# Two transformer blocks on one core: who sums the modulation, where latents and keys are turned, and in which order the mixers' outputs are normed

## The reference

```
c_act = silu(c)                                     # one row of 1024
mod   = c_act @ w_ada + b_ada                       # w_ada: 1024 x 6144
shift1, scale1, gate1, shift2, scale2, gate2 = split(mod, 6)
h     = rms_norm(x, g_mix) * (1 + scale1) + shift1
q_a, lat, k_r, iq, ik, iw, q_b, k_b, v_b, f_b = split(h @ w_in)
o_a   = dsa_attention(rope(q_a), rms_norm(lat, g_kv), rope(k_r), rope(iq), rope(ik), iw)
        # index scores: sum over 8 heads of iw * relu(iq . ik); the best 128 keys are kept
o_b   = forgetting_attention(q_b, k_b, v_b, f_b + b_forget)
mixed = concat(rms_norm(o_a, g_out_a), rms_norm(o_b, g_out_b))
x     = x + gate1 * (mixed @ w_out)
x     = x + gate2 * peer(rms_norm(x, g_ffn) * (1 + scale2) + shift2)
out   = rms_norm(x, g_final)
```

## Time and profile before

| | |
|---|---|
| runs | 3534.08, 3538.93, 3541.27 us; median 3538.93 |
| the profiled execution | 3541.71 us, its span 3539.9 |
| granted TensorE clock, mean | 0.972 |
| busy: TensorE, weight loads, VectorE, ScalarE, GpSimd | 94, 83, 76, 40, 29% |
| DMA | 855.56 MB, 242 GB/s over the span |

### The profile page before, as it was taken

One profiled execution on the slowest core, in us unless ns is written; L12 is line 12 of the kernel. 1 busy time (PEld: TensorE's weight loads), 2 busy tenths in 40 slices (PEclk: granted clock), 3 DMA queues, 4 the chain that ended last, 5 costly groups with the idle time before them and its releaser, 6 DMA issues. The chain is left out here.

```text
span 3539.9 us, 46446 instructions
## 1 busy us (share of the span) xinstructions
PE 3338.2 (94%) x18703; PEld 2946.8 (83%) x18703; DVE 2672.7 (76%) x4561; ACT 1400.4 (40%) x1899; POOL 1031.9 (29%) x652
## 2 busy tenths in 40 slices
PE   8997899999999998999999899889999999999998
PEld 7967558889999898788887786789999898888887
DVE  4458654349999895788888497549999896788888
ACT  4322452233333574233333345333333575333333
POOL 6516700002444330333332000002443331333332
PEclk9998999999999999999999899899999999999999
DMA  6313313237898899899997120226888899999996
GB/s 227 108 51 140 109 54 119 90 99 263 301 326 306 297 345 326 321 359 360 363 360 276 54 72 7 84 73 240 313 314 311 290 349 326 350 362 359 360 361 248
DMA packets 330506, 855.56 MB, mean 242 GB/s; under 512 B 22258, under 2 KB 188066, under 8 KB 297139
## 3 DMA queue, kind: packets, MB, share of 16 engines
q1 hardware_dynamic: 256562, 584.12, 47.1%
q0 software_dynamic: 73728, 268.47, 20.7%
HBM read 746.58 MB, written 105.93 MB: 241 GB/s over the span
## 5 line engine op out<-in xcount | busy, mean ns | idle before, releaser
L293 PE MATMUL ps<-ht_hi,parts 128*128 128x384 f32 (+2 forms) x5088 | 1373.8, 348 | 38.5 <-DVE parts L276 38.1
L276 DVE TENSOR_TENSOR parts<-ring,parts 128x2048 fp32r<-128x2048 f32 (+1 forms) x317 | 741.9, 2340 | 357.0 <-ACT parts L268 356.7
L293 PEld LDWEIGHTS ps<-ht_hi,parts 128*128 128x128 f32 x5088 | 936.6, 191 | 85.7 <-DVE parts L276 48.9
L268 ACT ACTIVATE parts<-ring 128x2048 fp32r<-128x2048 f32 (+1 forms) x317 | 606.7, 1914 | 831.7 <-PE ps L1525 677.2
L293 PE MATMUL ps<-ht_lo,parts 128*128 128x384 f32 (+2 forms) x2544 | 877.5, 345 | 0.0
L1888 POOL DMA_INDIRECT scr<-in_p_rows_u,cst x256 | 403.3, 1575 | 885.9 <-DVE scr L1758 563.9
L335 ACT ACTIVATE scr<-ps 128x384 f32<-128x384 f32 (+2 forms) x497 | 244.4, 505 | 942.0 <-PE ps L293 879.6
L1888 POOL DMA_INDIRECT scr<-in_peer_v,cst x256 | 375.3, 1466 | 770.2 <-DVE xres L1775 620.3
L1525 PE MATMUL ps<-parts,ht_lo 128*128 128x512 f32 x2304 | 530.2, 390 | 6.5 <-DVE ht_lo L1852 6.5
L1525 PE MATMUL ps<-parts,ht_hi 128*128 128x512 f32 x2304 | 529.3, 390 | 4.5 <-DVE ht_hi L1852 4.5
L1525 PEld LDWEIGHTS ps<-parts,ht_lo 128*128 128x128 f32 x2304 | 434.4, 189 | 97.3 <-DVE ht_lo L1852 6.9
(11 more groups left out here) (255 smaller groups left out, 2787.4 us busy)
## 6 DMA issues: line engine op xcount, KB each, us to landing
ring<-in_peer_u SPq DMA_DIRECT2D x128, 1024.0 KB, 6.8
ring<-in_peer_v SPq DMA_DIRECT2D x128, 1024.0 KB, 7.5
hbuf<-scr SPq DMA_DIRECT2D x128, 384.0 KB, 7.0
gbuf<-scr SPq DMA_DIRECT2D x96, 512.0 KB, 8.6
scr<-gbuf SPq DMA_DIRECT2D x64, 768.0 KB, 9.3
scr<-hbuf SPq DMA_DIRECT2D x64, 768.0 KB, 11.9
ring<-in_w_in SPq DMA_DIRECT2D x35, 1024.0 KB, 5.4
xres<-in_w_ada SPq DMA_DIRECT2D x18, 1024.0 KB, 7.4
```

What stands on the lines that cost most here:

```text
L268: e.activation(halves(m)[0], slot_view(m)[:, 0:units[m][0]], ACT.Copy).then_inc(A.sem, A.up(("hi", m)))
L276: e.tensor_tensor(lo, slot_view(m)[:, 0:units[m][0]], hi.bitcast(F32), ALU.subtract).then_inc(V.sem, V.up(("lo", m), ("slot", m)))
L293: ins = e.matmul(ps, l, r, start=(i == 0), stop=(i == n - 1))
```

## The change

**Modulation.** w_ada is laid out anew, as 6 groups of 1024 columns by 8 chunks of 128 rows: 48 pieces of 128x1024 (0.5 MB). Of a group VectorE multiplies piece 0 by a column of c and adds the other seven with one instruction each (`ada_dve`); eight matmuls of one column then sum over the partitions (`ada_pe`), and the bias is added a group at a time (`ada_sums`). Pieces 0 to 23 go with the eight units gq 0 to gv 3, three a unit; 24 to 47 with gb 0 to wo 2, two to four a unit, one beside each of wb. On VectorE they stand right behind the split of the next unit. GpSimd has no part of it, and the sliding stage none either. A load waits for the piece four before it.

**Mixers.** The positions come first on SP's queue, the sines and angles behind unit m2 0, latents' squares, index queries, latents and keys beside qa 0, the queries' rotation behind qa 1, and their turned copies behind the first block of index scores.

**Norm of the outputs.** Squares, root and turn by block: the squares of blocks 3, 2, 1 and 0 at iterations 11, 13, 15 and 17 of the loop, three roots at 16. wo2 0 takes the blocks as 3, 2, 1, 0; the loads of x and gate wait for the last scores instead of the last output.

```
-            for s in range(ADA_2):  ada_pool(e, w, s)          # gla_pool; sliding_pool likewise
+        ADA_GLA = {("gq", 0): (0, 3), ("gq", 1): (3, 6), ("gk", 0): (6, 9), ("gk", 1): (9, 12),
+                   ("gv", 0): (12, 15), ("gv", 1): (15, 18), ("gv", 2): (18, 21), ("gv", 3): (21, 24)}
+        ADA_JOIN = {("gb", 0): (24, 26), ("gb", 1): (26, 30), ("gb", 2): (30, 34), ("gb", 3): (34, 38),
+                    ("wb", 0): (38, 39), ("wb", 1): (39, 40), ("wb", 2): (40, 41), ("wb", 3): (41, 42),
+                    ("wo", 0): (42, 44), ("wo", 1): (44, 46), ("wo", 2): (46, 48)}
+        def ada_load(e, w, s):
+            if s >= 24:      w.wait_ge(*at_point("pv_pe", NB - 1))
+            if s % 24 >= 4:  w.wait_ge(*at_point("ada_used", s - 4))
+            e.dma_start(ada_in(s), inp["w_ada_2"][s])...
+        def ada_dve(e, w, span):
+            for s in range(*span):
+                cc = s % NC
+                w.wait_ge(*at_point("c_act")); w.wait_ge(*at_point("ada", s))
+                if cc == 0:
+                    if s % 24: ada_sums(e, w, s // NC - 1)
+                    ins = e.tensor_scalar(acc, ada_in(s), ct[:, 0:1], None, ALU.mult)
+                else:
+                    w.wait_ge(*V.now())
+                    ins = e.scalar_tensor_tensor(out=acc, in0=ada_in(s), scalar=ct[:, cc:cc + 1], in1=acc, ...)
+                ins.then_inc(V.sem, V.up(("ada_used", s)))
+        def ada_pe(e, w, k):
+            ps = bank(w, ("mods", k))
+            w.wait_ge(*at_point("ada_used", 8 * k + 7))
+            for j in range(8):  e.matmul(ps[:, j:j + 1], ada_acc(8 * k)[:, 128 * j:128 * j + 128], one, ...)
 # gla_pe, join_pe: where TensorE sums the groups
                     cols_major(e, w, (name, s, 0), v, 0)
+                    if (name, s) == ("gk", 0):  ada_pe(e, w, 0)
                     cols_major(e, w, (name, s, 1), v, 128, ("used", m))
+                    if (s, blk) == (1, 1):  ada_pe(e, w, 1)     # gv
+                    if (s, blk) == (3, 2):  ada_pe(e, w, 2)     # gv
+                if s == 2:  ada_pe(e, w, 3)                     # gb, between its two halves
+                if s == 1:  ada_pe(e, w, 4)                     # behind wb 1
+                    if (s, blk) == (2, 2):  ada_pe(e, w, 5)     # wo
 # gla_dve (gk, gv and join_dve likewise)
                     split_lo(e, w, U[name, s] + 1)
+                    ada_dve(e, w, ADA_GLA[name, s])
                     put_dve(e, w, (name, s, 1), dst[:, 2 * s + 1, :], psum((name, s, 1)), (name, "dve"))
 # mixers_dve
-            angles_dve(e, w)
             for (name, s), n, dst in m2_parts:
                 split_lo(e, w, U[name, s] + 1)
+                if (name, s) == ("qa", 0):  turned_keys(e, w)   # rotations of iq, k_r, ik; latents; copies
                 for blk in (1, 3):
                     put_dve(...)
+                if (name, s) == ("m2", 0):  angles_dve(e, w)
 # mixers_act: sines behind split_hi in m2 1, latent_squares in qa 0, and
+                if i in (11, 13, 15, 17):  mixed_squares(e, w, 3 - (i - 11) // 2)
+                if i == 16:
+                    for blk in (3, 2, 1):  mixed_root(e, w, blk)
 # mixed_pe
+            for blk in (3, 2, 1):  mixed_turn(e, w, blk)
+            for blk in (3, 2, 1, 0):
+                w.wait_ge(*at_point("ht", "mix", blk))
+                rows_major(e, w, ("wo2", 0, blk), v, 256, blk, ...)
+                if blk == 3:  mixed_turn(e, w, 0)
 # mixed_act
+            mixed_high(e, w, 3)
+            mixed_root(e, w, 0)
+            for blk in (2, 1, 0):  mixed_high(e, w, blk)
 # mixed_dve
+            for blk in (3, 2, 1):  mixed_mean(e, w, blk)
+            for blk in (3, 2, 1):  mixed_row(e, w, blk)
+            mixed_low(e, w, 3)
+            mixed_mean(e, w, 0)
+            mixed_row(e, w, 0)
+            for blk in (2, 1, 0):  mixed_low(e, w, blk)
```

More of the change, by code:

```diff
@@ L542, in ada_pool @@
[L542 to L570, removed]
@@ new lines, in ada_loads @@
+        def ada_loads(e, w, span):
+            for s in range(span[0] + 4, span[1] + 4):
+                if s // 24 == span[0] // 24:
+                    ada_load(e, w, s)
+        def ada_dve(e, w, span):
+            for s in range(*span):
+                cc = s % NC
+                acc = ada_acc(s)
+                w.wait_ge(*at_point("c_act"))
+                w.wait_ge(*at_point("ada", s))
+                if cc == 0:
+                    if s % 24:
+                        ada_sums(e, w, s // NC - 1)
+                    ins = e.tensor_scalar(acc, ada_in(s), ct[:, 0:1], None, ALU.mult)
+                else:
+                    w.wait_ge(*V.now())
+                    ins = e.scalar_tensor_tensor(out=acc, in0=ada_in(s), scalar=ct[:, cc:cc + 1], in1=acc, op0=ALU.mult,
+                                                 op1=ALU.add)
+                ins.then_inc(V.sem, V.up(("ada_used", s)))
@@ new lines, in ada_sums @@
+        def ada_sums(e, w, k):
+            cols = slice(8 * k, 8 * k + 8)
+            w.wait_ge(*at_point("ps", ("mods", k)))
+            w.wait_ge(*at_point("ada_bias"))
+            e.tensor_tensor(md[:, cols], psum(("mods", k))[:, 0:8], bd[:, cols], ALU.add).then_inc(
+                V.sem, V.up(("free", ("mods", k)), ("mod_done",)))
+        def ada_pe(e, w, k):
+            ps = bank(w, ("mods", k))
+            w.wait_ge(*at_point("ada_used", 8 * k + 7))
+            for j in range(8):
+                ins = e.matmul(ps[:, j:j + 1], ada_acc(8 * k)[:, 128 * j:128 * j + 128], one, start=True, stop=True)
+            ins.then_inc(P.sem, P.up(("ps", ("mods", k))))
@@ L580, in ada_turn @@
         def ada_turn(e, w):
-            for part in range(2):
-                w.wait_ge(*at_point("mod_done", part))
+            w.wait_ge(*at_point("mod_done"))
             ps = bank(w, ("modt",))
             e.transpose(ps[0:48, 0:128], md, ident).then_inc(P.sem, P.up(("ps", ("modt",))))
-        U = number
         def gla_sp(e, w):
@@ L2227, in mixers_act, with latent_squares @@
                     ins.then_inc(A.sem, A.up(("exp2", i)))
+                if i in (11, 13, 15, 17):
+                    mixed_squares(e, w, 3 - (i - 11) // 2)
+                if i == 16:
+                    for blk in (3, 2, 1):
+                        mixed_root(e, w, blk)
+        def latent_squares(e, w):
+            w.wait_ge(*at_point("m2", "act"))
+            w.wait_ge(*at_point("m2", "dve"))
+            for blk in range(NB):
+                if blk:
+                    w.wait_ge(*A.now())
+                e.activation(SCW[:, 0:128], M2[:, blk, 0:128], ACT.Square, accum_out=ssl[:, blk:blk + 1]).then_inc(
+                    A.sem, A.up(("squares", "lat")))
+            root_act(e, w, "lat", ssl)
         def latent_act(e, w, i):
@@ L2451, in mixed_act, with mixed_mean, mixed_row @@
             for s in range(4):
                 split_hi(e, w, U["wo2", s] + 1)
[L2454 to L2456 removed]
+        def mixed_mean(e, w, blk):
+            s = ssm[:, 2 * blk:2 * blk + 2]
+            w.wait_ge(*at_point("squares", "mix", blk))
+            e.tensor_scalar(s, s, 1.0 / 512, EPS, ALU.mult, ALU.add).then_inc(V.sem, V.up(("mean", "mix", blk)))
+        def mixed_row(e, w, blk):
+            s = ssm[:, 2 * blk:2 * blk + 2]
+            w.wait_ge(*at_point("root", "mix", blk))
+            e.reciprocal(s, s).then_inc(V.sem, V.up())
@@ L2467, in mixed_dve @@
-            mixed_low(e, w, NB - 1)
+            for k in range(2):
+                mv = MIX[:, blk, 512 * k:512 * k + 512]
+                e.scalar_tensor_tensor(out=mv, in0=mv, scalar=s[:, k:k + 1], in1=go[:, 512 * k:512 * k + 512],
+                                       op0=ALU.mult, op1=ALU.mult).then_inc(V.sem, V.up(("mix_normed", blk)))
+        def mixed_dve(e, w):
+            for blk in (3, 2, 1):
+                mixed_mean(e, w, blk)
+            for blk in (3, 2, 1):
+                mixed_row(e, w, blk)
+            mixed_low(e, w, 3)
+            mixed_mean(e, w, 0)
+            mixed_row(e, w, 0)
+            for blk in (2, 1, 0):
+                mixed_low(e, w, blk)
```

282 lines of the change are left out of this document (134 added, 148 removed).

## The result

| | before | after |
|---|---|---|
| median of 4 runs | 3536.5 us (3529.9 to 3541.3) | 3481.0 us (3480.2 to 3485.5) |
| ratio | | 0.9847, 95% interval 0.9828 to 0.9866 |
| the profiled execution, its span | 3541.7, 3539.9 us | 3481.2, 3479.4 us |
| granted TensorE clock, mean | 0.972 | 0.982 |

What follows compares the result with a forecast made beforehand. TensorE, busy 94% of the span, was taken as the bound, with time won only at its waits and low clock. Gains 25.9 + 16.5 + 12.8 = 55.2 off 3541.7, less 2.8, gave 3483.7, said as 3483; range 3465 to 3502 (0.67).

Steps and rivals of the forecast that it cites:

- The step for (gk, 0): First projections: TensorE stands still 7.6 us for VectorE's eighth modulation sum; with 3.0 of low clock, a loss of 10.6.
- (gb, 2): Join: the fourth group of column sums waits 2.1 us for VectorE, 3.1 with low clock (0 to 5).
- (gr, 1): The wait for GpSimd at 140 us goes, a 5.5 us wait for this unit's split comes; gain 1.5 (0 to 5).
- The sliding stage: Without GpSimd's sums and their DMAs: projections 100.4 to 71.4 us, gain 29.0; attention blocks gain 16.7.
- The low clock behind the stalls: First projections and join: 3.0 us lost behind the 7.6 us wait, 1.0 behind the 2.1 us wait.
- VectorE's 48 instructions: First projections and join: 58 us of sums on VectorE, costing nothing as such beside TensorE's work, 58 without that cover.
- Mixers: Latents and keys turned beside the query units: first relu from 2022.24 to 2002.9 us; gain 16.5 (10 to 18).
- Norm by blocks: Norm of the mixers' outputs: first wo2 matmul comes 14.3 us earlier; gain 12.8 (7 to 15).
- b: VectorE becomes the bound in the sliding projections and beside (qa, 0): gain 20 less, 3504 us (3502 to 3520); chance 0.19.
- c: Whole kernel: more comes back, no clock is lost behind the new waits, 3460 us; chance 0.06.
- d: First projections and join: w_ada loads delay the units' weights if DMA carries under some 160 GB/s, 3551 us; chance 0.04.
- e: First projections and join: DMA traffic, not GpSimd, stretches VectorE, 1 us in each of 17 units, 3500 us; chance 0.04.

Runs made afterwards that it cites:

- sum_early: Changed kernel with w_ada pieces 6 and 7 summed ahead of the four gate instructions, piece 8 alone in (gk, 0)'s iteration: 3467.8 us, 0.9804 to before.
- best: sum_early plus (gr, 1)'s split ahead of exps and products, and the fourth column sums behind (gb, 2): 3456.3 us, 0.9771 to before.
- pool_light: Kernel before, GpSimd doing only the last add of each sliding-stage modulation step; loads, waits and column matmuls stay: 3497.1 us, ratio 0.9887.
- pool_busy: Changed kernel with GpSimd's products and halvings put back as idle work on leftovers, without loads; gates' products of n=2 and 3 wait: 3535.5 us.
- dve_extra: Changed kernel with 5.2 us of idle VectorE work behind each split in the iterations of sqkv 1 to 5: 3505.4 us.
- m_only: Kernel before with only the modulation part of the change: median 3515.2 us, ratio 0.9936.
- l_only: Kernel before with only the mixers' latents and keys part of the change: median 3523.6 us, ratio 0.9959.
- n_only: Kernel before with only the norm by blocks: median 3525.5 us, ratio 0.9964.

## Why the prediction was right

**The new stalls by order came out to the tenth.** The step for (gk, 0) went through VectorE's queue: gate instructions to 59.8, split to 63.2, two sums to 65.8, TensorE from 58.2: 7.6 us. The timelines of VectorE and TensorE after:

```profile
57.26 2.53 DVE L764 SCALAR_TENSOR_TENSOR scr<-ps,scr 128x512 f32<-128x512 f32 x4 [8.88 <-ACT scr L716]
60.90 2.29 DVE L276 TENSOR_TENSOR parts<-ring,parts 128x2048 fp32r<-128x2048 f32 x1 [1.11 <-ACT parts L268]
63.31 2.69 DVE L548 SCALAR_TENSOR_TENSOR scr<-xres,scr 128x1024 f32<-128x1024 f32 x2
```
```profile
66.05 3.57 PE L564 MATMUL ps<-cst,scr 128*128 128x1 f32 x16 [7.55 <-DVE scr L548]
69.48 0.77 PE L293 MATMUL ps<-ht_hi,parts 128*128 128x512 f32 x1
```

In (gb, 2) it is 2.15 us for 2.1 predicted, before (gr, 1) 4.9 for 5.5, with 3.4 us at half clock behind it, 1.7 us of work, where I had taken off 3.2, so that step gave 3.6 instead of 1.5. sum_early shows that the first stall comes from VectorE's order alone; in best, moving one split and one group of column sums took the other two away.

**The sliding stage**: right in mechanism (pool_light, pool_busy), though what the prediction calls stretching is waiting for GpSimd's instruction, and an input in SBUF is not enough for it; 3.7 us too careful in the projections. The 2.7 that I had added to 68.7 for the thin margin were not there: 67.7. VectorE's margin of 1 us a unit is 0.9 in dve_extra, with 2.7 once at the start; since the splits take 2.3 us again, it suffices. In the attention block n=2 is 42.0 instead of 40.1, n=0 and 1 together 70.7 instead of 73.

**The low clock behind the stalls was mis-sized**, the one term that erred against the forecast. I took 3.0 us behind the wait of 7.6 and 1.0 behind that of 2.1, and 1.8 us for a group of 16 one-column matmuls. At full clock a group takes 1.8 to 1.95, in the two stalled places 3.57 and 3.20, and the clock stays at half beyond it: granted 0.67 in the first of the windows below (69.48 to 77.76 us, behind the first group) and 0.68 in the second (the group in (gb, 2) and what follows).

```profile
69.48:77.76 8.28, 8.28 (x26) 0.67 0.32 111
...
514.80:525.60 10.80, 10.73 (x41) 0.68 0.74 254
```

The stall in (gb, 2) cost 7.4 us with its group, not 4.9; that is most of the join's 3.4 too little. The window from 141 us from which I took the 3.0 held only the end of a group of 4; for the 1.0 I had no row. Of the 1.7 too little up to (gr, 0), 1.5 is the low clock behind the group in (gv, 1), told in the last section. There the sum also has a slip: up to (gr, 0) the kernel before has 3.9 us of one-column matmuls (12 in 1.4, five times 4 in 0.5), not 3.1, so the +2.0 should have been about 1.4.

**VectorE's 48 instructions** cost nothing beyond the two stalls, as predicted: its instructions of 128x1024 take 1.28 us, those with a scalar product alone 0.74 (0.75 taken).

**Mixers**: no idle before (m2, 1); the first relu 42.7 us after the end of (m2, 0), 43 predicted, 62.7 before:

```profile
1978.34 0.66 ACT L2162 ACTIVATE scr<-ps 128x256 f32<-128x256 f32 x2
```

Of the 1.2 us that I had taken off for waits and low clock only 0.1 came.

**Norm by blocks**: 5.5 us from the last attention matmul to wo2's first, 6 predicted. The turns begin 1.2 us behind it and take 4.3:

```profile
2198.53 4.26 PE L329 MATMUL ps<-cst,scr 128*128 128x128 f32 x24 [1.20 <-DVE scr L2496]
2202.78 0.50 PE L293 MATMUL ps<-parts,ht_hi 128*128 128x256 f32 x2
```

The first matmul came 14.5 us earlier (14.3 predicted); what was too careful is the 1.5 that I had taken off for the turn of block 0 and low clock inside the unit: (wo2, 0) takes 12.6 us, 0.9 less than before. The table load took 1.28 us again, and the three roots began 0.01 behind it, as in the earlier trace rows; the 2.66 us that the Trainium skill (ScalarE: Activation LUTs, What ACT_TABLE_LOAD costs) gives for a switch do not show in this place either.

```profile
2195.33 1.28 ACT L2468 ACT_TABLE_LOAD   x1
2196.62 0.39 ACT L2468 ACTIVATE scr<-scr 128x2 f32<-128x2 f32 x3
```

**The rivals.** b stayed away: in the sliding projections by 0.9 us a unit, and beside (qa, 0) no wait for it showed. c would have needed stalls without low clock; they had more of it. d: TensorE waits for no landed unit up to 680 us, and in the join, from 500.1 to 512.9 us, 273 GB/s flow. e: pool_light refutes it.

The errors partly cancelled: 10 us too careful at (gr, 1), in the sliding stage, the mixers and the norm, 6 too cheap in the new stalls and groups. So the mechanism was right, but that the median came within 2 us of 3483 is in part luck: by the traces the sum of -55.2 was 5.3 off, and the profiled execution before lay 5.2 us over the median where I took off 2.8. What the two expert layers added and lost (+1.7, -3.0) has no edit behind it: block one's moved by -4.2 to +0.3 us in m_only, l_only, n_only and pool_light too.

## What to carry to other kernels

Work moved off GpSimd can cost nothing on VectorE although VectorE is the busier, if VectorE's instructions had been waiting for GpSimd's: compare the longest and the median of equal instructions before counting busy time. When work is inserted in a hand-written order, follow the one instruction that TensorE will ask for through its engine's queue; that gave each new wait to 0.1 us here, though not the low clock behind it, and the repair (two sums ahead of a wait instead of behind it) was worth 12 us. Price a stall of TensorE with the low clock behind it, for short matmuls that follow it too: the 2.15 us of waiting in (gb, 2) cost 5.5 beside the group's own 1.9.

## What the runs showed of the hardware that was not expected

- A group of 16 one-column matmuls without any wait can be followed by the lower clock: behind the one in (gv, 1), at 106.0 us, the granted clock was 0.5 from 109.1 to 112.5, and the unit took 1.5 us longer; behind those in (gv, 3), (wb, 1) and (wo, 2) it stayed at full speed, and in the last version the one in (gv, 1) had none behind it either. What decides this stays open.
- With GpSimd at work back to back a split of 2.28 us took up to 5.69, the same longest as before: it loses what is left of the GpSimd instruction under way, in these traces up to 3.4 us. A unit has a dozen instructions that can lose so, and TensorE waited 11.3 us at one place. A GpSimd product begun during a split loses too: two took 5.59 and 5.67 us there instead of 3.6.
